# A PEER decoder block on one core: row 5 in two parts, the best expert's row first, and pair 0's dots and adds moved

## What is computed

```
q  = h2 @ w_q                      # 8 heads x 2 halves x 128
sc = q . sub_keys                  # 16 lists of 128 scores per token
s1,i1 / s2,i2 = top 16 of each list
cand = s1[:,None] + s2[None,:]     # 256 sums per head, ids i1*128 + i2
top_s, pos = top 16 of cand;  eid = cand_id[pos];  g = softmax(top_s)
a = u_tab[eid] . h2;  y = sum over 128 experts of g * gelu(a) * v_tab[eid]
x = x + gate2 * y
```

## Time and profile before

| | |
|---|---|
| median of 3 runs | 904.86 us (904.42 to 905.25) |
| profiled execution | 903.49 us |
| its span in the profile | 901.7 us |
| granted TensorE clock | 0.984 of full speed |
| busy: PE, DVE, ACT, POOL | 772.4, 613.4, 346.9, 287.8 us |
| read from HBM | 335.11 MB, 268.45 MB of it by GpSimd's queue |

### The profile page before, as it was taken

How to read it: one execution, slowest core, us unless ns; L and a number is a source line. 1 busy time by engine, 2 the same in 40 slices (tenths; PEclk the granted TensorE clock), 3 DMA queues, 4 the chain that set the end, 5 groups by cost and what they waited for, 6 DMA issues and landing times.

```text
span 901.7 us, 8442 instructions
## 1 busy us (share of the span) xinstructions
PE 772.4 (86%) x2526; PEld 416.1 (46%) x2526; DVE 613.4 (68%) x1420; ACT 346.9 (38%) x1027; POOL 287.8 (32%) x279
## 2 busy tenths in 40 slices
PE   4999999999999999999997778687777777777777
PEld 2477777667556556565652333233322233222232
DVE  6788798954587967748669788768744444444445
ACT  3457688862144342422423242322422222222222
POOL 4000000000244444554636444353343334333320
PEclk9999999999999999999999989999999999999999
DMA  9977545679399999999999999999999999999995
GB/s 373 421 281 280 186 188 200 264 301 379 120 372 422 411 423 421 422 419 422 421 420 423 420 423 420 422 423 419 423 420 423 420 423 420 421 422 422 422 421 205
DMA packets 43812, 336.70 MB, mean 373 GB/s; under 512 B 4852, under 2 KB 4980, under 8 KB 7032
## 3 DMA queue, kind: packets, MB, share of 16 engines
q0 software_dynamic: 37152, 268.45, 71.9%
q1 hardware_dynamic: 6600, 67.72, 18.9%
q10 hardware_dynamic: 16, 0.00, 0.0%
HBM read 335.11 MB, written 1.05 MB: 373 GB/s over the span
## 4 chain that ended last, share of the span: by engine, by line
PE 47%; DMA 36%; DVE 10%; ACT 3%; issue 2%; POOL 1%; SPq 0%; DVEq 0%; ACTq 0%
DMA ring<-in_peer_uv,eid 26%; PE ps_y L1611 21%; DMA rows<-in_peer_uv,eid 6%; PE bank L1581 5%; DMA extra<-in_peer_uv,eid 4%; PE bank L1547 3%; DVE ring L1010 3%; PE bank L1422 2%; PE bank L1424 2%; PE bank L1423 2%; PE bank L1562 2%; PE ps_y L1422 1%; PE ps_y L1386 1%; PE ps_y L1424 1%; PE ps_y L1423 1%
## 5 line engine op out<-in xcount | busy, mean ns | idle before, releaser
L1611 PE MATMUL ps_y<-ring,diag 128*128 128x512 f32 x572 | 273.2, 617 | 58.2 <-ACT diag L1297 58.2
L581 POOL DMA_INDIRECT ring<-in_peer_uv,eid x142 | 150.1, 1057 | 414.8 <-DVE eid L916 227.0
L1010 DVE CUSTOM_DVE_ANT_0 ring<-ring,gates 128x1024 f32<-128x1024 f32 x143 | 173.2, 1224 | 101.8 <-DMA ring<-in_peer_uv,eid 101.0
L1611 PEld LDWEIGHTS ps_y<-ring,diag 128*128 128x128 f32 x572 | 108.0, 194 | 204.5 <-issue 116.8
L1285 ACT ACTIVATE mask<-mask 128x2 f32<-128x2 f32 (+1 forms) x132 | 26.7, 203 | 376.3 <-DVE mask L1010 376.1
L1297 ACT ACTIVATE diag<-ident,mask 128x128 f32<-128x128 f32 x256 | 87.3, 386 | 0.3
L1611 PE MATMUL ps_y<-rows,diag 128*128 128x512 f32 x136 | 63.8, 613 | 9.6 <-ACT diag L1297 9.6
L1290 ACT ACTIVATE mask<-g_sb,mask 128x1 f32<-128x1 f32 x256 | 61.9, 287 | 4.3
L1010 DVE CUSTOM_DVE_ANT_0 rows<-rows,gates 128x1024 f32<-128x1024 f32 x34 | 41.3, 1225 | 32.2 <-DMA rows<-in_peer_uv,eid 32.1
L645 DVE TENSOR_TENSOR w_lo<-ring,w_hi 128x512 fp32r<-128x512 f32 x76 | 50.6, 685 | 10.0 <-PE bank L1424 8.7
L1106 ACT ACTIVATE w_hi<-ring 128x512 fp32r<-128x512 f32 x76 | 45.6, 626 | 22.5 <-PE bank L1424 22.0
(11 more groups left out here) (228 smaller groups left out, 1194.0 us busy)
## 6 DMA issues: line engine op xcount, KB each, us to landing
ring<-in_ada_t SPq DMA_DIRECT2D x11, 2048.0 KB, 9.6
ring<-in_in_t SPq DMA_DIRECT2D x10, 2048.0 KB, 10.1
ring<-in_up_t SPq DMA_DIRECT2D x2, 2048.0 KB, 8.7
ring<-in_out_t SPq DMA_DIRECT2D x2, 2048.0 KB, 13.7
kz<-in_peer_t SPq DMA_DIRECT2D x2, 2048.0 KB, 17.7
ring<-in_peer_uv,eid POOLq DMA_INDIRECT x142, 29.0
x_sb<-in_x SPq DMA_DIRECT2D x2, 1024.0 KB, 12.0
ring<-in_ada_t SPq DMA_DIRECT2D x2, 1024.0 KB, 21.3
```

What stands on the lines that cost most here:

```text
L581: pool.indirect_dma_start(uv_row(n), None, peer_uv, bass.IndirectOffsetOnAxis(ap=eid[:, n:n + 1], axis=0)).then_inc(s_uv[name], 16)
L1010: dve.tensor_tensor_reduce(u_row(n), u_row(n), h2[:, n // P, :], 1.0, 0.0, ALU.mult, ALU.add, adot[:, at:at + 1]).then_inc(s_dot, 1)
L1611: ins = pe.matmul(ps_y[:, cut], diag[:, n % ND, :], v_row(n)[:, cut], start=first, stop=last)
```

## The change

There are four edits. (1) Row 0's id is made from the best key of each list, right after their indices, and GpSimd waits for that alone; the first maxima are read from PSUM, and ScalarE copies the scores afterwards. (2) Row 5 gets no place of the ring: its u goes to the second tile's half of `yT`, its v to the second half of the score buffer `sc`, by two indirect DMAs of 4 KB to a partition, which wait for the fourth up product; R1a and R1b take rows 10 and 11, W and X rows 12 and 13, and rows 8 and 9 go into R2a and R2b behind rows 0 and 1. (3) On VectorE the shift of the top scores, dot 0, the scaling of the gates and dot 1 stand ahead of `choose_experts(0, 0)`. (4) On TensorE the adds of pair 0 stand between output products 0 and 1 of tile 1.

```diff
@@ -70,6 +70,8 @@
+PARTED = 5
@@ -87,8 +89,8 @@
-BUFFERS = [("R2a", 0), ("R2b", 0), ("R3a", 0), ("R3b", 0), ("G", 0), ("R0a", 0), ("R0b", 0), ("R1a", 0),
-           ("R1b", 0), ("W", 11), ("X", 12), ("V", 52), ("S", 53), ("E", 76), ("Ka", 88), ("Kb", 89)]
+BUFFERS = [("R2a", 0), ("R2b", 0), ("R3a", 0), ("R3b", 0), ("G", 0), ("R0a", 0), ("R0b", 0), ("R1a", 10),
+           ("R1b", 11), ("W", 12), ("X", 13), ("V", 52), ("S", 53), ("E", 76), ("Ka", 88), ("Kb", 89)]
@@ -96,6 +98,9 @@
     for n in range(ROWS):
+        if n == PARTED:
+            table.append(("parts", 0, None))
+            continue
...
@@ -311,14 +317,18 @@
+        parted_u = yT[:, 1].rearrange("p g b n -> p (g b n)")
+        parted_v = sc[:, LISTS * P // 2:LISTS * P]
...
@@ -561,11 +576,23 @@
             for n in range(ROWS):
                 name, fills, held = table[n]
+                if n == PARTED:
+                    await_item(pool, ("up", 1, 1, 1))
+                    pool.wait_ge(s_parted_id, 2)
+                    pool.indirect_dma_start(
+                        u_row(n), None, halves,
+                        bass.IndirectOffsetOnAxis(ap=parted_id[:, 0:1], axis=0)).then_inc(s_parted_u, 16)
...
+                    continue
...
                 if n == 0:
+                    pool.wait_ge(s_best, 1)
+                elif n == 1:
                     pool.wait_ge(s_eid, 1)
                 elif n == EARLY:
                     pool.wait_ge(s_eid, 2)
@@ -889,14 +916,19 @@
             def choose_first():
-                await_read(dve, ("sc", 0, 0))
+                key = ("sc", 0, 0)
+                await_item(dve, key)
                 for l in range(2):
-                    ins = dve.max(v16[:, l, 0:EARLY], sc[:, l * P:(l + 1) * P])
+                    ins = dve.max(v16[:, l, 0:EARLY], bank(key)[:, l * P:(l + 1) * P])
...
+                ins.then_inc(s_first, 1)
+                dve.wait_ge(s_first, 1)
                 link(dve.tensor_copy(i16f[:, 0:2, 0:EARLY], i16[:, 0:2, 0:EARLY]))
+
+                dve.scalar_tensor_tensor(out=eid[:, 0:1], in0=i16f[:, 0, 0:1], scalar=float(P),
+                                         in1=i16f[:, 1, 0:1], op0=ALU.mult, op1=ALU.add).then_inc(s_best, 1)
...
@@ -913,8 +945,12 @@
-                dve.scalar_tensor_tensor(out=eid[:, 0:EARLY], in0=pf[:, 0:EARLY], scalar=float(P),
-                                         in1=pf[:, EARLY:2 * EARLY], op0=ALU.mult, op1=ALU.add).then_inc(s_eid, 1)
+                dve.scalar_tensor_tensor(out=eid[:, 1:EARLY], in0=pf[:, 1:EARLY], scalar=float(P),
+                                         in1=pf[:, EARLY + 1:2 * EARLY], op0=ALU.mult, op1=ALU.add).then_inc(s_eid, 1)
+                dve.wait_ge(s_eid, 1)
+                for part in range(2):
+                    dve.tensor_scalar(parted_id[:, part:part + 1], eid[:, PARTED:PARTED + 1], 2.0, float(part),
+                                      ALU.mult, ALU.add).then_inc(s_parted_id, 1)
@@ -1039,13 +1093,18 @@
             choose_keys(0, 0)
             choose_pairs(0, 0)
+            shift_best(0, 0)
+            dots(0, (0,))
+            scale_gates(0, 0)
+            dots(0, (1,))
             choose_experts(0, 0)
...
             for pair in range(NG * PAIRS):
-                dots(pair)
+                if pair:
+                    dots(pair)
@@ -1265,6 +1324,10 @@
                     if t:
                         act.wait_ge(s_eid, m + 2)
+                    elif m == 0:
+                        act.wait_ge(s_first, 1)
+                    elif m == 5:
+                        act.wait_ge(s_added, PARTED + 1)
@@ -1604,6 +1667,8 @@
                     pe.wait_ge(s_diag, n + 1)
+                    if n == PARTED:
+                        pe.wait_ge(s_parted_v, 16)
@@ -1634,9 +1699,10 @@
             for h in range(2):
                 turn_wide(1, h)
-            for n in range(2):
-                out_part(1, n)
-            for pair in range(NG * PAIRS):
+            out_part(1, 0)
+            add_rows(0)
+            out_part(1, 1)
+            for pair in range(1, NG * PAIRS):
                 for stage in behind.get(pair, ()):
```

More of the change, by code:

```diff
@@ L290, in block_kernel @@
         late_id = sb("late_id", [P, 2, SPLIT], I32)
+        parted_id = sb("parted_id", [P, 2], I32)
         adot = mask[:, 0:2 * TOPK]
@@ L317, in u_row @@
         def u_row(n):
-            return uv_row(n)[:, 0:D]
+            return parted_u if n == PARTED else uv_row(n)[:, 0:D]
         def v_row(n):
-            return uv_row(n)[:, D:2 * D]
+            return parted_v if n == PARTED else uv_row(n)[:, D:2 * D]
         halves = peer_uv.rearrange("r (a d) -> (r a) d", d=D)
@@ L395, in block_kernel @@
         s_warm = sem("root_of_one_ready")
+        s_first = sem("first_scores_ranked")
+        s_best = sem("best_expert_id_ready")
         s_g0 = sem("top_scores_shifted")
@@ L399, in block_kernel @@
         s_uv = {name: sem(f"uv_landed_{name}") for name, _ in BUFFERS}
+        s_parted_id = sem("parted_row_ids_ready")
+        s_parted_u = sem("parted_row_u_landed")
+        s_parted_v = sem("parted_row_v_landed")
         s_late_id = sem("late_part_ids_ready")
@@ L563, in _ @@
                 name, fills, held = table[n]
+                if n == PARTED:
[4 more added lines that the diff above has]
+                        bass.IndirectOffsetOnAxis(ap=parted_id[:, 0:1], axis=0)).then_inc(s_parted_u, 16)
+                    pool.indirect_dma_start(
+                        v_row(n), None, halves,
+                        bass.IndirectOffsetOnAxis(ap=parted_id[:, 1:2], axis=0)).then_inc(s_parted_v, 16)
+                    continue
                 if held is None:
@@ L890, in choose_first @@
             def choose_first():
-                await_read(dve, ("sc", 0, 0))
+                key = ("sc", 0, 0)
+                await_item(dve, key)
                 for l in range(2):
-                    ins = dve.max(v16[:, l, 0:EARLY], sc[:, l * P:(l + 1) * P])
+                    ins = dve.max(v16[:, l, 0:EARLY], bank(key)[:, l * P:(l + 1) * P])
                 link(ins)
                 for l in range(2):
-                    ins = dve.max_index(i16[:, l, 0:EARLY], v16[:, l, 0:EARLY], sc[:, l * P:(l + 1) * P])
-                link(ins)
+                    ins = dve.max_index(i16[:, l, 0:EARLY], v16[:, l, 0:EARLY], bank(key)[:, l * P:(l + 1) * P])
+                ins.then_inc(s_first, 1)
+                dve.wait_ge(s_first, 1)
                 link(dve.tensor_copy(i16f[:, 0:2, 0:EARLY], i16[:, 0:2, 0:EARLY]))
+                dve.scalar_tensor_tensor(out=eid[:, 0:1], in0=i16f[:, 0, 0:1], scalar=float(P),
+                                         in1=i16f[:, 1, 0:1], op0=ALU.mult, op1=ALU.add).then_inc(s_best, 1)
                 sums8 = flat[:, 0:EARLY * EARLY]
@@ L941, in choose_pairs, with gates_of, shift_best, scale_gates @@
                 top16(lambda l: tv[:, l, :], lambda l: p3[:, l, :], lambda l: cd[:, l, :], nh)
+            def gates_of(t, n):
+                h, nh = GROUPS[t][n]
+                at = t * P + h * TOPK
+                return nh, g_sb[:, at:at + nh * TOPK].rearrange("p (h k) -> p h k", k=TOPK)
+            def shift_best(t, n):
+                nh, gt = gates_of(t, n)
+                tp = tv[:, 0:nh, :]
+                dve.tensor_tensor(gt, tp, tp[:, :, 0:1].to_broadcast([P, nh, TOPK]),
+                                  ALU.subtract).then_inc(s_g0, 1)
+            def scale_gates(t, n):
+                nh, gt = gates_of(t, n)
+                dve.wait_ge(s_g1, group_no[t, n] + 1)
+                link(dve.tensor_reduce(gsum[:, 0, 0:nh], gt, AX_X, ALU.add))
+                link(dve.reciprocal(gsum[:, 1, 0:nh], gsum[:, 0, 0:nh]))
+                link(dve.tensor_tensor(gt, gt, gsum[:, 1, 0:nh].unsqueeze(2).to_broadcast([P, nh, TOPK]), ALU.mult))
             def choose_experts(t, n):
@@ L946, in choose_experts @@
                 nk = nh * TOPK
-                tp = tv[:, 0:nh, :]
                 at = t * P + h * TOPK
-                gt = g_sb[:, at:at + nk].rearrange("p (h k) -> p h k", k=TOPK)
-                dve.tensor_tensor(gt, tp, tp[:, :, 0:1].to_broadcast([P, nh, TOPK]),
-                                  ALU.subtract).then_inc(s_g0, 1)
+                if not t == n == 0:
+                    shift_best(t, n)
                 ps = pos[:, 0:nk]
@@ L978, in choose_experts @@
                                          op0=ALU.mult, op1=ALU.add).then_inc(s_eid, nh)
[L979 to L982, removed]
+                if not t == n == 0:
+                    scale_gates(t, n)
             behind = {}
@@ L1003, in run, with dots @@
                     stage()
-            def dots(pair):
-                for n in (2 * pair, 2 * pair + 1):
-                    dve.wait_ge(s_uv[table[n][0]], 16 * (table[n][1] + 1))
+            def dots(pair, which=(0, 1)):
+                for n in (2 * pair + a for a in which):
+                    if n == PARTED:
```

(3 more changed lines are left out.)

## The result

The kernel with the change takes **909.99 us** (median of 4, 908.06 to 910.81), the kernel before, beside it, 904.82 (904.42 to 905.25): ratio 1.0055, 95% interval 1.0043 to 1.0067, so **5.2 us slower**. Repeated later (experiment 9) it is 910.37 against 905.01, ratio 1.0056 (1.0043 to 1.0069). The profiled execution of the kernel after is its fastest, 908.06 us with a span of 906.2; before it was 903.49 and 901.7. The two spans thus differ by 4.5 us, and the medians by 0.7 to 0.9 more.

A forecast was written before the change was run, and what follows sets the result against it. DMA's gather of expert rows, full at 420 to 421 GB/s from 264 to 884 us, bounds the kernel; 4.0 us of delay less 1.0 of reserve gives +3.0 on 904.86, so 907.9 us, range 905.2 to 910.1.

The forecast's parts named there:

- rival C: Rows 16 to 28: emptied DMA queues restart slowly, adding 1.8 us to +3.0, so +4.8, 909.7 us; chance 0.12.
- Early issues: GpSimd's first gathers go earlier, ten rows with DMA by 257; the lead is used up at row 25.
- list of signs: Five signs for the changed profile: first gathers, TensorE's idleness, VectorE's stall, row 16 and pair 4, DMA loss 283 to 315.
- TensorE between the output products: TensorE idles 1.3 us for diag 0, then 3.44 us of adds; output product 1 ends at 263.0, 4.8 us later.
- VectorE's stall: Ahead of output part 1, VectorE stands 4.0 us, from 259.3 until output product 1 is read at 263.25.
- It passes on whole to pair 4: The 4.0 us reach row 16 (283.9) and pair 4 (287.1) whole; TensorE's wait for diag 8 absorbs nothing.
- the reserve at row 25 is 6.8 - 5.8 = 1.0 us: At row 25's gather, an issue up to 1.0 us late costs nothing, cutting the 4.0 us delay to +3.0.
- the clock: TensorE's granted clock around pair 4: the prediction had no term for it.
- Rival A: A gather into an empty queue takes 4.3 us, so row 25 has 2.5 us reserve: +1.5, 906.4 us; chance 0.14.
- Rival B: Later output product does not pass on to pair 4, early issues stay won: -2.8, 902.1 us; chance 0.14.

The follow-up runs named there:

- experiment 9: Kernel after, unaltered, timed and profiled again against the kernel before: 910.37 us, ratio 1.0056.
- Experiment 1: Kernel after with only pair 0's adds put back behind output product 1: 905.10 us, ratio 1.0005.
- 7: Kernel after with row 5 whole again and the buffers in the old order: 910.21 us, ratio 1.0054.
- experiment 2: Kernel before with three dummy VectorE operations (2.16 us) between dots 2 and 3 and output part 1: 906.99 us, ratio 1.0027.
- experiment 10: Kernel after with three dummy products on TensorE where it waits for diag 8 ahead of pair 4: 908.36 us, ratio 1.0038.
- 3: Kernel before with six dummy VectorE operations (4.34 us) between dots 2 and 3 and output part 1: 911.15 us, ratio 1.0073.
- experiment 5: Kernel after with pair 0's adds behind output product 1, R1a and R1b given to rows 8 and 9, dot 4 in norm 2's root gap: 904.21 us.
- experiment 6: Kernel before with only dot 4 moved into VectorE's gap during norm 2's root: 904.72 us, ratio 0.9999.
- experiment 11: The kernel of experiment 5 with head 1's expert step behind pair 2 in place of pair 3: 906.80 us, ratio 1.0018 against the kernel before.
- experiment 8: Kernel before with three dummy VectorE operations behind ids 16 to 31, ahead of dots 8 and 9: 910.02 us, ratio 1.0050.
- experiment 12: Kernel before with two dummy products on TensorE where it waits 1.73 us for diag 8: 904.63 us, ratio 1.0000.

## Why the prediction was right in sign and short in size

The sign and the mechanism held, step by step. The range (905.2 to 910.1) held the first median, 909.99, at its edge, and not the second, 910.37. That it held the first is in part luck: its upper end came from rival C, and the clock that adds to the loss stood in no term. The forecast itself, 907.9, is 2.1 to 2.5 us short.

- **Early issues.** Forecast: row 0 at 235.6, row 2 still at 242.7, the halves of row 5 at 246.4 and 247.7, row 8 at 255.8. Measured: 235.97, 242.82, 246.54 and 247.78, 255.78. That their lead is worth nothing once the later issues are late was said, and two experiments bear it out: 1 (most of the early issues without the delay, no gain) and 7 (286 GB/s in place of 385 from 240 to 264, no change). Where the lead goes was misplaced: not at row 25, but from 264 to 283, where the later row 12 left 2.8 us empty that the list of signs did not have.
- **TensorE between the output products.** Forecast: 1.3 us of idleness, adds at 252.7. Measured: 1.10 by the line, adds at 252.74.
- **VectorE's stall.** Forecast 4.0 us, ended at 263.25. Measured 3.87, at 263.35. Experiment 1 takes it away and the loss with it.
- **It passes on whole to pair 4.** Forecast 287.1 and row 16 at 283.9. Measured 287.18 and 283.95; TensorE's wait ahead of pair 4 absorbed nothing, it grew from 1.73 to 2.65.
- **The step that failed: "the reserve at row 25 is 6.8 - 5.8 = 1.0 us".** It took the shortest landing in the trace, 5.8 us, for what every gather takes at a hole, and it looked at row 25 alone. The line is late before row 25. In experiment 2 row 16 took 8.5 us at its hole as before and gave nothing back; in experiment 10 it took 6.4 and gave 2.1 us back, and by row 21 the line was late by 4.7, more than the issues. For 2.16 and 4.34 us of pure delay the profiled spans grew by 2.7 and 4.2. With the 1.0 us gone the sum is 4.0 and not 3.0; in the profiled execution, where the clock stayed full in this stage, it was 4.5. Why a gather at a hole takes 6.4 us in one execution and 8.5 in another stays open.
- **A term left at nothing: the clock.** Forecast: nothing said, since the earlier trace rows has a granted clock of 1.00 there. The longer wait ahead of pair 4 brings TensorE to 0.50 in some executions, for 1.7 us more, and that can account for the 0.7 to 0.9 us by which the medians differ more than the two profiled spans. The sizes do not add up exactly: the filler took 2.0 us off the median, and the 3.4 us of loss that it left (2.4 to 4.6 by the interval) hold the forecast's 3.0 as well as a loss without reserve. That the reserve is missing rests on experiments 2 and 3, not on this one. Two executions of the changed kernel were profiled, one with a fall (912.03 us) and one without (908.06). How many of the others had one is read from their spread alone and stays open.
- **Rival A** (a gather into an empty queue in 4.3 us, so more reserve) falls: the dummies would then have cost nothing up to 2.16 us. The rule on which it leaned, in the Trainium skill's page "DMA: Bandwidth & Descriptors", section "Anatomy of one DMA — SWDGE (gpsimd) path", would give, as an estimate, 4.4 us for such a row; the shortest landing of a row found in these traces is 5.4 us (row 2 of experiment 5), and the measurement decides.
- **Rival B** (faster) falls with TensorE's wait, as above.
- **Rival C** (909.7, restarts of an emptied queue) names nearly the right time, and it is not refuted. The end moved by more than the issues (4.5 against 4.05, 2.5 against 2.16), and in experiment 10 row 16 gave 2.1 us back while rows 17 to 21 lost 2.8, which is a kept reserve with losses behind it, as C has it; in experiment 2 row 16 gave nothing back and row 21 lost 0.8 more. No run here separates "no reserve" from "a reserve, lost again by restarts". Both leave the line late by the whole delay, and the rest is clock.

## What to carry to other kernels

The reserve of a transfer is not its latency less the shortest latency seen anywhere. Its time at a hole varied from 5.4 to 8.5 us here, so measure the reserve by a known delay, as experiments 2 and 3 do, and look at the first issues behind the delay, not at the one with the smallest number. Where DMA sets the end, bytes brought early are worth nothing if the next issues come later; and later issues moved forward alone (0.65 us in experiment 6) won nothing either. Work put on an engine ahead of what another engine waits for has the price of that whole wait: pair 0's adds, 3.4 us of TensorE, cost nothing extra in one place and 5 us in the other.

## What the hardware showed that I had not expected

- TensorE's granted clock fell to 0.50 behind a wait of 2.66 us in one execution and stayed full behind 2.65 us in another of the same program; it fell behind 2.24 us (experiment 11) and 3.92 us (experiment 8, 6.43 us for 3.70 us of work), and in experiment 12 a filler for the wait of 1.73 us gained nothing. A wait that "costs nothing" on an engine that is nearly always busy can thus cost more than its length.
- The time of one gather from issue to landing, where the gap to the landing before it shows a hole, is not one number: 5.6 us for row 21 of experiment 8, 5.8 for row 8 of experiment 1, 6.4 for row 16 of experiments 9 and 10, 8.2 for row 21 and 8.5 for row 16 of experiment 2. The length of the issuing instruction does not tell them apart: it was 1.78 to 1.79 us for row 16 in all three executions.
- GpSimd's issue instruction takes 0.93 to 0.95 us in most places, and for rows 16 to 18 mostly 1.78 to 1.99 us while VectorE's dots run one after another. The Trainium skill's "GPSIMD Engine Reference" says, under "Key points", that this engine "Shares its SBUF interfaces with VectorE", with contention from instructions that read two inputs from SBUF; the dots do, and most rows of the trace agree. But row 18 of experiment 8 took 0.96 us and row 17 of experiment 9 0.94 us beside the same dots, so that this alone does not settle the length.
